# Operands of the three-pass products moved to 192 modulo 256 bytes in SBUF, the weights left at 128

## What is computed

```
# first_block, for each of 2 layers
h = rms_norm(x);  p = h @ w_in                     # 1024 x 12388, all branches' inputs and gates
o = [dsa, mla, diff, sgu, memory](p)               # five branches, each 512 x 512
mixed = sum(sigmoid(merge_n) * ((o_n * silu(gate_n)) @ w_branch_n))
x = x + mixed @ w_out
# second_block, layer 0 on 512 tokens and 256 context tokens, layer 1 on 512 at its end
h = rms_norm_2(x) * (1 + scale) + shift
x = x + g1 * (na_mixer(h) or hgrn2_mixer(h))       # na_w_qkv, na_w_o or hg_w_in, hg_w_o
h = rms_norm_2(x) * (1 + scale2) + shift2
x = x + g2 * (silu(h @ w_a) * (h @ w_u)) @ w_out   # D_FF = 2816
```

## The kernel before

| pair | used by | matmuls of three-pass products | place before | place after |
|---|---|---|---|---|
| xF | first block, all branches | 3696 of 512 columns, 2496 of 256, 192 of 228 | 192 | 192 |
| og, ten times | `branch_tail` | 96 of 512 each | 0, 32, 64, 96, 128; 160, 192, 224, 64 (320), 128 (384) | 192 (448) |
| b_ckv, b_cq | latent attention | 96 of 512, 144 of 384 | 0 | 192 (448) |
| e_mem | memory branch | 384 of 256 | 0 | 192 (448) |
| na_x | neighbourhood mixer, in | 1728 of 256 | 160 | 192 (448) |
| na_oF | neighbourhood mixer, out | 192 of 512, 192 of 256 | 160 | 192 (448) |
| ffn_h_0 | feed-forward 0, in | 1056 of 512, 1056 of 256 | 192 | 192 (448) |
| ffn_g_0 | feed-forward 0, out | 528 of 512, 528 of 256 | 0 | 192 (448) |
| hg_h | gated scan, in | 768 of 512, 960 of 256 | 128 | 192 (448) |
| hg_og | gated scan, out | 192 of 512 | 128 | 192 (448) |
| ffn_h_1, ffn_g_1 | feed-forward 1 | 1056 and 528 of 512 | 64, 96 | 192 (448) |

## Time and profile before

### The profile page before, as it was taken

How to read it: one execution, slowest core, us unless ns; L and a number is a source line. 1 busy time by engine, 2 the same in 40 slices (tenths; PEclk the granted TensorE clock), 3 DMA queues, 4 the chain that set the end, 5 groups by cost and what they waited for, 6 DMA issues and landing times. The chain is left out here.

```text
span 4183.5 us, 56453 instructions
## 1 busy us (share of the span) xinstructions
PE 3927.9 (94%) x23092; PEld 3329.1 (80%) x23092; DVE 1647.3 (39%) x3386; ACT 1443.3 (34%) x2330; POOL 1397.4 (33%) x517
## 2 busy tenths in 40 slices
PE   6999989999899899999989999999999889889999
PEld 5777878887777788788769988888888778767877
DVE  5834152322483524332261454311114566664111
ACT  3434242342243423334232364221112454433221
POOL 2211323343321132234322321223222567643442
PEclk8899999999989999999999999999999999999999
DMA  3221414434222142344411210212212111103332
GB/s 115 56 82 42 135 54 142 118 116 126 75 56 80 41 129 64 119 123 134 135 52 61 74 24 21 61 51 75 61 52 65 42 51 44 48 11 93 93 97 70
DMA packets 476077, 323.12 MB, mean 77 GB/s; under 512 B 31450, under 2 KB 472237, under 8 KB 475821
## 3 DMA queue, kind: packets, MB, share of 16 engines
q1 hardware_dynamic: 422112, 268.18, 22.3%
q10 hardware_dynamic: 53708, 51.33, 3.6%
HBM read 315.74 MB, written 2.16 MB: 76 GB/s over the span
## 5 line engine op out<-in xcount | busy, mean ns | idle before, releaser
L95 POOL TENSOR_TENSOR w_lo<-w_raw,w_hi 128x2048 fp32r<-128x2048 f32 (+6 forms) x329 | 1155.9, 3518 | 2506.6 <-ACT w_hi L227 2506.1
L227 ACT ACTIVATE w_hi<-w_raw 128x2048 fp32r<-128x2048 f32 (+3 forms) x278 | 471.9, 1698 | 1103.6 <-PE psum L263 1073.5
L261 PE MATMUL psum<-xF_hi,w_hi 128*128 128x512 f32 x1232 | 492.2, 400 | 21.9 <-ACT a_relud L1578 8.5
L263 PE MATMUL psum<-xF_hi,w_lo 128*128 128x512 f32 x1232 | 485.2, 394 | 0.0
L262 PE MATMUL psum<-xF_lo,w_hi 128*128 128x512 f32 x1232 | 483.5, 392 | 0.0
L261 PE MATMUL psum<-ffn_h_hi,w_hi 128*128 128x512 f32 (+1 forms) x1056 | 375.5, 356 | 2.7 <-issue 1.3
L263 PE MATMUL psum<-ffn_h_hi,w_lo 128*128 128x512 f32 (+1 forms) x1056 | 374.9, 355 | 0.0
L262 PE MATMUL psum<-ffn_h_lo,w_hi 128*128 128x512 f32 (+1 forms) x1056 | 374.2, 354 | 0.0
L261 PEld LDWEIGHTS psum<-xF_hi,w_hi 128*128 128x128 f32 x1232 | 232.9, 189 | 78.2 <-ACT a_relud L1578 10.2
L263 PEld LDWEIGHTS psum<-xF_hi,w_lo 128*128 128x128 f32 x1232 | 232.6, 189 | 51.8
L262 PEld LDWEIGHTS psum<-xF_lo,w_hi 128*128 128x128 f32 x1232 | 232.7, 189 | 48.7
(11 more groups left out here) (543 smaller groups left out, 8288.8 us busy)
## 6 DMA issues: line engine op xcount, KB each, us to landing
w_raw<-in_w_in_dram SPq DMA_DIRECT2D x56, 1024.0 KB, 5.3
ada_w<-in_ada_w_dram ACTq DMA_DIRECT2D x48, 1024.0 KB, 7.0
w_raw<-in_ffn_w_in_dram SPq DMA_DIRECT2D x88, 512.0 KB, 5.1
w_raw<-in_w_in_dram SPq DMA_DIRECT2D x78, 512.0 KB, 4.2
w_raw<-in_ffn_w_out_dram SPq DMA_DIRECT2D x32, 704.0 KB, 4.4
w_raw<-in_w_branch_dram SPq DMA_DIRECT2D x74, 256.0 KB, 4.5
w_raw<-in_hg_w_in_dram SPq DMA_DIRECT2D x32, 512.0 KB, 4.7
w_raw<-in_na_w_qkv_dram SPq DMA_DIRECT2D x12, 1024.0 KB, 5.1
```

The source lines that it names most:

```text
L95: return eng.tensor_tensor(pair.lo, src, pair.hi.bitcast(F32), ALU.subtract)
L227: act.activation(self.w(j).hi, self.raw_w(j), ACT.Copy).then_inc(*self.high_done.up(1))
L261: pe.matmul(out, left.hi, right.hi, start=first, stop=False)
L263: return pe.matmul(out, left.lo, right.hi, start=False, stop=last)
```

## The change

The table of ten places for og and the sizes written out for ffn_h, ffn_g and hg_h are dropped. `placed` now asks the allocator where the next tile would begin (`nc.sbuf_base`) and opens an unused tile that fills up to the next address that is 192 modulo 256. It is called ahead of every pair, also ahead of b_ckv, e_mem, xF, na_x, na_oF and hg_og, which had no call before. b_cq and ffn_g follow at the same place, since the sizes before them are multiples of 256. xF is there already and no tile is added for it. The instructions of all engines and their order are the same; other tiles that are opened after a pair shift by at most 576 bytes. Core of the diff:

```diff
-OG_AT = ((0, 32, 64, 96, 128), (160, 192, 224, 320, 384))
+OPERANDS_AT = 192
...
-def placed(nc, ctx, name, size):
-
-    if size:
-        ctx.enter_context(nc.sbuf_tensor(f"{name}_before", [P, size // 4], F32))
+def placed(nc, ctx, name):
+
+    gap = (OPERANDS_AT - nc.sbuf_base) % 256
+    if gap:
+        ctx.enter_context(nc.sbuf_tensor(f"{name}_before", [P, gap // 4], F32))
...
-        placed(C.nc, ctx, f"og_{C.serial}", (OG_AT[l][n] - 256) % 512)
+        placed(C.nc, ctx, f"og_{C.serial}")
         og = pair_of(C.nc, ctx, f"og_{C.serial}", [P, 4, SEQ])
...
+        placed(nc, keep, f"b_ckv_{l}")
         ckv = pair_of(nc, keep, f"b_ckv_{l}", [P, 2, SEQ])
...
+            placed(nc, tmp, f"e_mem_{l}")
             mem = pair_of(nc, tmp, f"e_mem_{l}", [P, KD, MEM])
...
+        placed(nc, ctx, "xF")
         C.xF = pair_of(nc, ctx, "xF", [P, KD, SEQ])
...
+            placed(nc, tmp, "na_x")
             normed = pair_of(nc, tmp, "na_x", [P, KD, 768])
...
+        placed(nc, ctx, "na_oF")
         oF = pair_of(nc, ctx, "na_oF", [P, KD, 768])
...
-        placed(nc, ctx, f"ffn_h_{l}", (192, 64)[l] - 416 + 512)
+        placed(nc, ctx, f"ffn_h_{l}")
         hN = pair_of(nc, ctx, f"ffn_h_{l}", [P, KD, T])
-        placed(nc, ctx, f"ffn_g_{l}", (0 - 192 + 512, 96 - 64)[l])
         gF = pair_of(nc, ctx, f"ffn_g_{l}", [P, FB // 2, T])
...
-        placed(nc, ctx, "hg_h", 128 - 416 + 512)
+        placed(nc, ctx, "hg_h")
         hN = pair_of(nc, ctx, "hg_h", [P, KD, 768])
...
+        placed(C.nc, ctx, "hg_og")
         self.og = pair_of(C.nc, ctx, "hg_og", [P, HGH, SEQ])
```

## The result

| | before | after |
|---|---|---|
| median of 8 runs each | 4190.44 us (4178.45 to 4195.57) | 4173.69 us (4159.22 to 4176.12) |
| ratio | | 0.9953, 95% interval 0.9935 to 0.9971 |
| profiled execution: time, span | 4185.28, 4183.5 us | 4176.12, 4173.6 us |

What follows compares the result with a forecast made beforehand. TensorE, busy 94% of the span, was taken as the bound: number of matmuls times their distance, set by operand placement. Terms summed to 22.8 us, 4185.3 to 4162.5 profiled; forecast median 4159 us, range 4145 to 4173.

Steps and rivals of the forecast that it cites:

- Item 1: Feed-forward 1: ffn_h_1 from 64 and ffn_g_1 from 96 to 192, 4.0 ns per 512-column matmul; 4.2 and 2.1 us gained.
- Item 3: na_x from 160 to 192, 1728 matmuls of 256 columns at 114.6 instead of 118.3 ns; 6.4 us, bounds 0.5 and 8.5.
- rival A: All newly placed 256-column products take the slow cadence; gain only 11.7 us, time 4171; chance 0.10.
- Item 2: ffn_g_0 from 0 to 192, 528 pairs of matmuls; 3.1 us gained, 1.3 if slow cadence alone, 3.7 if quick.
- Item 4: na_oF from 160 to 192: 0.7 us gained on 256-column products, 0.6 us on 512-column products.
- Items 5 and 6: Scan: hg_h from 128 to 192 gains 2.5 us at 256 columns (bounds 0, 6.2); hg_og and hg_h lose 1.3 at 512.
- the reason given for halving: Scan, hg_h: of 5.0 us only 2.5 counted, since TensorE would partly wait longer for other engines at the next level.
- Item 7: og, ten tiles at ten places all to 192, 960 matmuls at 2.5 ns less; 2.4 us gained.
- Item 8: e_mem from 0 to 192 gains 1.5 us; b_ckv and b_cq from 0 to 192 gain 0.6 us.
- B: Slow cadence takes new 256-column products and also today's quick ones in xF and ffn_h_0, 12.1 us back; 4183; chance 0.03.
- C: Placement is inert and distances differ because of what runs beside them; time stays at 4183; chance 0.06.
- D: Place modulo 512 counts, not 256; pairs at 448 could be bad, 21 us slower, 4204; chance 0.03.

Runs made afterwards that it cites:

- the third: The changed kernel run a third time without edit, on another set's chip as base for two later runs: 4171.82 us, ratio 0.9958.
- four variants: Changed kernel with everything shifted 64 bytes (0.9951); pairs at 192 modulo 512 (0.9943); ffn_g_0 alone at 0 (4177.50 us); og, hg_og, ffn_h_1, ffn_g_1 at 128 (0.9944).
- both sweeps: Changed kernel with ten extra short matmuls of varied widths ahead of products in na_x and each ffn_h_0 half, two width orders: 4164.57 and 4164.93 us.
- a variant: Changed kernel with og, hg_og, ffn_h_1 and ffn_g_1 at 128 modulo 256, the place of their weights: 4166.57 us, ratio 0.9944.
- the run at 64: Changed kernel with every pair at 64 instead of 192 modulo 256, weights at 128: 4209.67 us, ratio 1.0043.

## Why the prediction was right, point by point

**What bounds the kernel**: the distance between matmuls, and it goes with the placement. The runs bear this out: 512 columns in feed-forward 1 follow each other at 233.3 ns with the operand 64 or 32 behind the weights, at 226.7 with both at one place, and at 228.9 with it 64 ahead, but for one half stage in nine profiles; and moving the operands to the wrong side of the weights made the kernel slower than before.

| item | predicted, us | profiled execution | other executions of after |
|---|---|---|---|
| 1 ffn_h_1, ffn_g_1 | 6.3 | 7.0 | 7.0; 3.5 in the third |
| 2 ffn_g_0 | 3.1 | 2.0 | 2.0; 3.4 in the third |
| 3 na_x | 6.4 | 0.9 | 0.9, 0.9 |
| 4 na_oF | 1.3 | 0.7 | |
| 5 and 6 the scan | 2.5 - 1.3 | 2.8 | 1.5, 4.0 |
| 7 og | 2.4 | 2.4 | |
| 8 e_mem, b_ckv, b_cq | 2.1 | 1.2 + 0.2 | |
| ffn_h_0 | 0 | -2.6 | -2.6; 0.5 in the third |
| xF | 0 | -2.9 (512), -1.0 (256) | -0.9; 0 in the third |

The column of the profiled execution adds up to 10.7 us, and 3.7 of clock by the estimate above make 14.4, near the 14.8 us of the three-pass sum.

**Item 1** was mis-sized by a tenth: 4.4 ns (233.3 to 228.9 clean) and not 4.0, since the count in a stretch gave xF 229.9.

**Item 3 failed.** The step was "a quarter slow: 114.6", the mix that one execution showed at 192, carried over to an operand that had not been there. In all three profiles of after na_x ran slow in nearly all of its 1728 matmuls (117.7 ns), which is rival A's price. Of the four variants with the same distance to the weights and no extra matmuls, one was slow and three quick, 8.1 us. In one of these, and in both sweeps up to the first extra matmul, everything ahead of na_x was as in after: with the three profiles of after that is three times slow and three times quick for one and the same instructions and places. Both ends of the stated bounds, 0.5 and 8.5, occurred, and the value between them did not.

**ffn_h_0**, costed at nothing, lost 2.6 us in the profiled execution. Its second half turned slow, and so it did in the repeated kernel before. The prediction read that half as a fixed property.

**xF**, costed at nothing too, lost 2.9 us to the second cadence of 512 columns and 1.0 us to the slow one of 256 (its first stretch, near 50 us). The prediction held that xF "keeps its own all along" on one stretch of 512 columns; at this width it allowed for no second cadence, in none of its terms and none of its rivals.

**Item 2** gained 2.0, between the slow and the quick bound (1.3 and 3.7): 512 columns fell from 232.3 to 229.3 ns and 256 from 118.6 to 117.8. **Item 4** is right for 512 columns and nil for 256, which were slow. **Items 5 and 6**: the scan gave 2.8 us, and -3 us on the mean of three profiles of after against two of before. As forecast, it gave 1 to 3 us; the waits for the factors did not grow (36.2 to 35.6 us), so the reason given for halving is not shown. The clean distances of after price the move at 576 x 4.3 + 384 x 3.5 = 3.8 us and not 5.0, with 0.6 us lost on 512 columns: 3.2 us, close to the 2.8 measured with nothing halved. The size was partly luck. hg_og went from 227.4 to 229.2 ns as item 6 said, 0.3 us. **Item 7** hit: 233.3 to 230.9 us, clean 231.86 to 228.98 ns. The product that took 2.58 us at 32 goes from 475.81 to 478.33, 2.52 us, in after:

```profile
475.81 0.39 PE L262 MATMUL psum<-og_hi,w_hi 128*128 128x512 f32 x1
...
478.33 0.40 PE L264 MATMUL psum<-og_hi,w_lo 128*128 128x512 f32 x1
```

**Item 8**: e_mem gained on its stationary side only (118.7 to 113.5), not where it moves (118.5 to 117.8). b_ckv became dearer by 0.9 ns and b_cq cheaper by 2.0, nearly nothing in sum.

**The rivals.** A is what the profiled execution shows for na_x, ffn_g_0, na_oF and the moving e_mem; over all executions it is a matter of chance. As a share of the time known then, A is 0.9972, the forecast 0.9943, and the median of 0.9953 lies between them; the profiled execution gained less than A's 11.7 us. B's mechanism was named with 0.03 because "xF's surroundings hardly change", which is no protection: 2.6 us went from ffn_h_0, 3.9 us from xF, and 6.6 us from xF in a variant. The loss of ffn_h_0 came in the unaltered kernel as well, so it is the execution's and not the change's. C is refuted by the run at 64. The Trainium skill ("SBUF - State Buffer", section "Who interferes with whom") calls the two read ports independent and has TensorE wait for nobody; the runs show one form of product at 226.7 ns with equal places and at 233.3 with the operand 64 behind, each time that it was run so in feed-forward 1, by nothing but the distance between two addresses, so the measurement decides against the rule as it was applied there. D is refuted by the run with 192 modulo 512. Where the prediction was lucky: items 1, 5 and 7 carried it, item 5 by a size that came out for another reason, and 9 us were open on cadences that the one trace of before could not settle.

## What to carry to other kernels

Where TensorE is the bound and each matmul has a weight load of its own, look at the place of the moving operand minus the place of the weights, modulo 256 bytes, and not at either alone; here equal places were the best for 512 columns (64 ahead cost 1% more or, in its slower cadence, 3%; 64 behind 3%) and the worst for 256. Read the start-to-start distance of each stage in more than one execution before giving a stage a price: two values at one placement are two cadences, and which one comes can differ the next time. A change of a few bytes is measured in its own stage, since the cadences of others move the total by more.

## What the runs showed of the hardware

For an fp32r product of 128 rows with a weight load for each matmul, at 2.4 GHz, from start to start:

| moving minus stationary, modulo 256 | 512 columns | 256 columns |
|---|---|---|
| 0 (512: feed-forward 1 at 128; 256: hg_h in before) | 226.7 ns; 229.2 in og's products of twelve | 119.6 to 119.9 |
| +64 | 228.9 or 233.3 | 113.3 or 117.8 |
| -64 | 233.3 | 113.4 or 117.8 |
| -32 (before, ffn_g_1 and na_x) | 233.3 | 118.3 |
| 128 (before, ffn_g_0 and e_mem) | 232.3 | 118.5 to 118.7 |

The two cadences of 256 columns differ by 4.4 ns, 4%. In what was seen, which one holds changed where a stretch begins or at other matmuls in between, down to a single odd one; it stays for hundreds of matmuls, and it passed from ffn_h_0 to ffn_g_0 in every profile that has both 64 ahead. The two cadences of 512 columns at 64 ahead differ by 4.4 ns as well and last as long. Some operands always have the same one (in all profiles with the pairs 64 ahead of the weights, e_mem 117.8 where it moves and 113.5 where it is stationary), others change between executions of one kernel. The profile names no cause. That the reads of a weight load and of a running matmul meet in SBUF, and that the cadence is their relative phase, would fit all of this; it was only argued, not shown. Time at the lower clock ranged from 260.4 to 306.7 us over the profiles taken, with nothing in the placements to account for it; by estimate 46 us at half clock are 23 us lost, more than the 16.8 that the change gained.
